# Stick-breaking attention woven into a projection and MLP: the weights are turned into the score banks, and the pieces are regrouped

## The chip, the cores and the metric

The kernel runs on one NeuronCore of a Trainium2 chip. A time is the device time in microseconds (us) of one execution. The kernel before was run three times: median 2823.44, from 2823.38 to 2826.13. The profile is that of a further execution, which took 2821.06 us.

## The reference

One inference step of a layer with 2048 prompt tokens and 64 new tokens, model width 1024, in float32. The tokens are normalised and projected to four groups of heads; group C is stick-breaking attention, the part that the change is about. For one head:

```
def sb_block(qb, qpos, k, v, kpos):
    z = jnp.einsum('bqhd,bkhd->bhqk', qb, k) * (SB_DH ** -0.5)
    mask = kpos[None, :] < qpos[:, None]
    ls_neg = jax.nn.log_sigmoid(-z)
    ls_pos = ls_neg + z
    lneg = jnp.where(mask, ls_neg, 0.0)
    rest = lax.cumsum(lneg, axis=3, reverse=True) - lneg
    w = jnp.where(mask, jnp.exp(ls_pos + rest), 0.0)
    return jnp.einsum('bhqk,bkhd->bqhd', w, v)
...
mix = jnp.concatenate([o_a, o_b, o_c, o_d], axis=-1) @ w_out
x = x + g1 * mix
h2 = rmsnorm(x, ln2_g) * (1.0 + sc2) + sh2
x = x + g2 * (jnp.square(jax.nn.relu(h2 @ mlp_w1)) @ mlp_w2)
```

A key's weight is the sigmoid of its score times the product of `1 - sigmoid` of all later keys, so a scan along the keys stands where other attention has a softmax. There are four heads of width 64.

## The kernel before, in words

The program has two phases. Phase one (input projection, the other head groups, the attention of the first 512 tokens) is not touched. Phase two, the function `tail_phase`, does the output projection and the MLP for four blocks of 512 tokens (the last one of 576, in two groups of 256 and 320 columns), and during the first three blocks the attention of the next block, two heads at a time.

**Strips and tiles.** A matrix product in float32 is made of three products of rounded halves, on 128x512 tiles. A tile of the output projection (`out`) or of the MLP's first matrix (`hid`) is a *strip* of 8 x 3 = 24 matmuls (L2400, L2401, L2404); a tile of the second matrix (`prj`) is 6 matmuls (L2442 to L2444), or 12 at a block's end (`prj2`, L2465 to L2467). Tiles take the four PSUM banks `dn` in turn: tile `u` is written in `dn[u % 4]`, and the function `bank` lets TensorE wait until tile `u - 4` has been read out. ScalarE reads `hid` tiles (L2074 a relu, L2076 a square, after which VectorE makes the low half, L2252 and L2254); VectorE reads the others, adding them to the residual (L2220).

**Slots.** The order is written out by hand. Each strip has 4 slots, a `prj` tile 1, a `prj2` tile 2, so that a slot is 6 matmuls. Each engine walks the same list of tiles and calls `step(slot)` as it passes a slot; TensorE does the attention's pieces of a slot behind the slot's 6 matmuls, the other engines do the steps of all slots of a tile before they read that tile out.

**A pair** is one tile of 128 queries (64 for the new tokens) against up to 512 keys, both heads; there are 76 pairs in 8 groups, and a group's last pair ends with its output. Pair `t` begins at slot `beta[t]`, one each 10.75 slots. From there, in slots:

| slot | engine | work |
|---|---|---|
| 0 | TensorE | `score`: both heads' scores into the two banks `sc` (L2317) |
| 2 | ScalarE | two sigmoids of `sc` (L1948, L1949) |
| 5 | VectorE | copy, two scans, copy, product: the weights `taken` (L2133 to L2142) |
| 10, 12 | TensorE | `turn`: head 0, head 1 transposed into the one bank `wt`, 4 each (L2329) |
| 11, 13 | ScalarE | `copy`: `wt` into `aT` (L1956), which frees `wt` |
| 14, 15 | TensorE | `values`: head 0, head 1, weights times values into the bank `ob`, 8 matmuls each (L2340) |
| 17 to 23 | all | after a group's last pair: copy out, head norms, `turn_out` (slot 22, L2350, into `wt`), copy |

So the eight PSUM banks are 4 `dn`, 2 `sc`, 1 `wt`, 1 `ob`. In block 0 the weights are split into halves on the way (ScalarE L1940, VectorE L2123, 128x1024 each); later blocks load the halves from memory.

Of the kernel before, what the change touches and what calls it, by code (L numbers as in the profile page):

```python
# [1477 lines left out]
def tail_phase(nc, const, x_v, o_v, q_v, k_v, sbv_p, sbv_s, cache_sb_v, w_out, mlp_w1, mlp_w2, y_prompt, y_sample):  # L1478
# [8 lines left out]
    HALF = 2 * P  # L1487
    PV, PA = "dve", "act"

    def groups(b):  # L1490
# [31 lines left out]

    SIG, SCAN, TURN, COPY, VALUES = 2, 5, (10, 12), (11, 13), (14, 15)
    FIN_OUT, FIN_STAT, FIN_SCALE, FIN_TURN, FIN_COPY = 17, 18, 20, 22, 23
    LEAD = 6
    beta = [LEAD + 43 * i // 4 for i in range(N_PAIRS)]
    at = {slot: t for t, slot in enumerate(beta)}
    at_last = {beta[t]: t for t in range(N_PAIRS) if pairs[t].last}
    past_piece = {beta[t]: pairs[t].piece for t in range(N_PAIRS) if t + 1 == N_PAIRS or pairs[t].piece != pairs[t + 1].piece}
    N_SLOTS = beta[-1] + FIN_COPY + 2  # L1530
# [153 lines left out]

    wt_no = {}
    for slot in range(N_SLOTS):
        if slot - FIN_TURN in at_last:
            wt_no["fin", pairs[at_last[slot - FIN_TURN]].group] = len(wt_no)
        for j in range(2):
            if slot - TURN[j] in at:  # L1690
                wt_no["turn", at[slot - TURN[j]], j] = len(wt_no)

# [11 lines left out]
    with ExitStack() as ctx:  # L1704
# [31 lines left out]
        stage = strips[0:6]  # L1736
        dn = [ps(f"dn{i}") for i in range(4)]
        sc, wt, ob = ps("sc", (P, 2, 512)), ps("wt"), ps("ob")

# [44 lines left out]
        def _(sp):  # L1784
# [77 lines left out]
            def step(slot):  # L1862

                n = past_piece.get(slot - VALUES[1] - 1)
# [67 lines left out]
        def _(act):  # L1932
# [9 lines left out]
            def sigmoids(t):  # L1942
                p = pairs[t]
                act.wait_ge(sc_full, t + 1)
                wait(act, w_ready, t)
                wait(act, wt_full, wt_no["turn", t - 2, 1] + 1 if t >= 2 else 0)
                z = sc[0:p.rows, :, 0:p.w]
                act.activation(left[0:p.rows, :, 0:p.w], z, ACT.Sigmoid, scale=-1.0)  # L1948
                act.activation(taken[t % 2][0:p.rows, :, 0:p.w], z, ACT.Sigmoid).then_inc(sig_ready, 1)  # L1949

            def copy(t, j):
                p = pairs[t]
                act.wait_ge(wt_full, wt_no["turn", t, j] + 1)
                wait(act, pv_done, 2 * (t - 1) + j + 1)
                n = p.nk * p.rows
                act.activation(aT[0:p.kr, j, 0:n], wt[0:p.kr, 0:n], ACT.Copy).then_inc(wt_read, 1)  # L1956

# [16 lines left out]
            def place(g):  # L1974

                b, j = attn_groups[g]
                act.wait_ge(wt_full, wt_no["fin", g] + 1)
                wait(act, o_lo, KT * min(b, NB - 1))
                a, n = (BLK, DEC) if b == NB else (0, BLK)
                act.activation(oC[:, j, a:a + n], wt[:, 0:n], ACT.Copy, scale=prm2[:, R2_ON + 4 + j:R2_ON + 5 + j]  # L1980
                               ).then_inc(wt_read, 1)

            def step(slot):
                t = at_last.get(slot - FIN_COPY)
                if t is not None:
                    place(pairs[t].group)
                for j in range(2):
                    t = at.get(slot - COPY[j])
                    if t is not None:
                        copy(t, j)  # L1990
                t = at.get(slot - SIG)
                if t is not None:
                    sigmoids(t)
                t = at_last.get(slot - FIN_STAT)
                if t is not None:
                    head_roots(t)
# [40 lines left out]
            def inverse_rms(kind, b, g):  # L2037
                u = tile_no["nsum" if kind == "second" else "fsum", b, g]
                act.preload_act_table_set(EXP_LN)
                a, e = groups(b)[g]  # L2040
                act.wait_ge(d_full, u + 1)
                act.activation(rms[:, a:e], dn[u % 4][:, 0:e - a], ACT.Ln, scale=1.0 / D_MODEL,
                               bias=eps[:, 0:1]).then_inc(evac[PA], 1)
                act.wait_ge(evac[PA], freed[u][1])
                act.activation(rms[:, a:e], rms[:, a:e], ACT.Exp, scale=-0.5).then_inc(n_rms, 1)
# [14 lines left out]
            def hidden(b, c, ft, g):  # L2060
# [11 lines left out]
                if c == 0:  # L2072
                    act.wait_ge(lo2, KT * (b + 1))
                act.activation(r, dn[u % 4][:, 0:e - a], ACT.Relu).then_inc(evac[PA], 1)  # L2074
                act.wait_ge(evac[PA], freed[u][1])
# [27 lines left out]
            def rows_of(b, i, v):  # L2103
# [3 lines left out]
                wait(act, y_out[n % 2], 16 * (n // 2))  # L2107
                act.activation(yrow[n % 2][0:rows, 0:512], dn[u % 4][0:rows, :], ACT.Copy).then_inc(evac[PA], 1)

# [5 lines left out]
        def _(dve):  # L2115
# [98 lines left out]
            def added(kind, mod, b, f, g, u):  # L2214
# [3 lines left out]
                for s, t, m in ranges(a, e):  # L2218
                    cols = xs[b % 2][:, f, s:t]
                    ins = dve.scalar_tensor_tensor(out=cols, in0=dn[u % 4][:, s - a:t - a], scalar=modT[:, mod + f, m:m + 1],  # L2220
                                                   in1=cols, op0=ALU.mult, op1=ALU.add)
# [86 lines left out]
        def _(pe):  # L2308
            def score(t):
                p = pairs[t]  # L2310
                q, k = qp[p.group % 2], kp[p.piece % 2]
                wait(pe, sig_ready, t)
                pe.wait_ge(q_in[p.group % 2], 16 * (p.group // 2 + 1))
# [10 lines left out]
            def turn(t, j):  # L2324
                p = pairs[t]
                pe.wait_ge(w_ready, t + 1)
                wait(pe, wt_read, wt_no["turn", t, j])
                for v in range(p.nk):
                    ins = pe.transpose(wt[0:p.kr, v * p.rows:(v + 1) * p.rows],  # L2329
                                       taken[t % 2][0:p.rows, j, v * p.kr:(v + 1) * p.kr], ident[0:p.rows, 0:p.rows])  # L2330
# [14 lines left out]
            def turn_out(t):  # L2345
# [3 lines left out]
                for s in range(1 if p.sample else TPB):  # L2349
                    ins = pe.transpose(wt[:, s * p.rows:(s + 1) * p.rows], osb[0:p.rows, s * P:(s + 1) * P],  # L2350
                                       ident[0:p.rows, 0:p.rows])
                ins.then_inc(wt_full, 1)

            def step(slot):
                for j in range(2):
                    t = at.get(slot - VALUES[j])
                    if t is not None:
# [4 lines left out]
                for j in range(2):  # L2362
                    t = at.get(slot - TURN[j])
                    if t is not None:
                        turn(t, j)
# [150 lines left out]
```

## Time and profile before

| what | value |
|---|---|
| time, median of 3 (range) | 2823.44 us (2823.38 to 2826.13) |
| time of the profiled execution, its span | 2821.06 us, 2819.3 us |
| TensorE busy | 2718.6 us, 96% |
| VectorE busy, ScalarE busy | 1459.5 us, 1075.1 us |
| phase two | from 788.8 us to the end |
| stretch of phase two with attention and at full clock | 872 to 2245 us |

A row of the timeline has the start of an instruction (or of several alike in a row, xN) and how long it took. Matmuls overlap: the time of a matmul is read from its start to the next one's start, not from its own length. Idle time and what ended it stand in square brackets.

### The profile page before, as it was taken

The page shows a single profiled execution, that of the slowest core. Times are in us where ns is not written, and L with a number is a line of the kernel's source. Part 1 is how long each engine was busy: PE and PEld are TensorE (multiplying, and loading weights), DVE is VectorE, ACT ScalarE, POOL GpSimd, SP SyncE. Part 2 cuts the span into 40 slices and gives each one's busy share as a digit, 9 for nine tenths or more (in the row PEclk, how much of TensorE's full clock was granted, in tenths as well). Part 3 has the DMA queues.
Part 4 walks back from the last instruction along what each step waited for, and adds up shares of the span by engine and source line. Part 5 has one row for each costly group of instructions (what it writes and reads, how often), then busy time and mean ns, then how long its engine had stood idle before and what let it go on. Part 6 is the DMA issues. An engine that isn't in the chain of part 4 may idle for free.

```text
span 2819.3 us, 36506 instructions
## 1 busy us (share of the span) xinstructions
PE 2718.6 (96%) x14669; PEld 2224.5 (79%) x14669; DVE 1459.5 (52%) x2315; ACT 1075.1 (38%) x1728; POOL 33.2 (1%) x43
## 2 busy tenths in 40 slices
PE   7999999999978999999999999999999999999996
PEld 2589777777766777777787878777777788999996
DVE  4455563554436657665564455555545434544553
ACT  3374846656434343433433322343222322221112
POOL 0000000000000000000000000001000000100000
PEclk9999999999989999999999999999999999999999
DMA  9533435324386676775435454534453643454441
GB/s 338 174 105 114 115 113 153 113 83 135 101 282 244 221 243 227 238 253 206 147 138 192 179 185 164 191 127 172 151 204 140 216 180 135 165 177 166 166 179 64
DMA packets 285934, 485.99 MB, mean 172 GB/s; under 512 B 21963, under 2 KB 168326, under 8 KB 285766
## 3 DMA queue, kind: packets, MB, share of 16 engines
q1 hardware_dynamic: 279526, 471.07, 48.7%
q10 hardware_dynamic: 6240, 12.58, 1.2%
q8 instruction: 118, 1.93, 0.3%
q14 instruction: 50, 0.41, 0.0%
HBM read 374.52 MB, written 109.06 MB: 172 GB/s over the span
## 4 chain that ended last, share of the span: by engine, by line
PE 62%; DVE 5%; ACT 2%; DMA 2%; issue 1%; SPq 1%; DVEq 0%; ACTq 0%
PE t_dn L2400 10%; PE t_dn L2404 10%; PE t_dn L2401 10%; PE t_dn L2442 7%; PE t_dn L2444 7%; PE t_dn L2443 7%; PE t_ob L2340 3%; PE t_sc L2317 2%; PE t_wt L2329 2%; DVE t_left L2137 1%; PE t_dn L2465 1%; PE t_dn L2467 1%; PE t_dn L2466 1%; DVE t_xs L2220 1%; DMA ring_lo<-lo_scratch 1%
## 5 line engine op out<-in xcount | busy, mean ns | idle before, releaser
L2400 PE MATMUL t_dn<-t_h_hi,ring_hi 128*128 128x512 f32 (+2 forms) x1600 | 588.0, 368 | 18.0 <-ACT t_h_hi L2027 7.1
L2220 DVE SCALAR_TENSOR_TENSOR t_xs<-t_dn,modT,t_xs 128x512 f32<-128x512 f32 (+2 forms) x768 | 422.5, 580 | 312.9 <-PE t_dn L2444 167.6
L2404 PE MATMUL t_dn<-t_h_lo,ring_hi 128*128 128x512 f32 (+2 forms) x1600 | 568.9, 356 | 3.8 <-DVE t_h_lo L2202 3.4
L2401 PE MATMUL t_dn<-t_h_hi,ring_lo 128*128 128x512 f32 (+2 forms) x1600 | 566.6, 354 | 0.0
L2442 PE MATMUL t_dn<-t_g_hi,t_w2h 128*128 128x512 f32 (+2 forms) x1120 | 412.3, 368 | 11.5 <-DVE t_xs L2220 9.3
L2444 PE MATMUL t_dn<-t_g_lo,t_w2h 128*128 128x512 f32 (+2 forms) x1120 | 396.6, 354 | 0.0
L2443 PE MATMUL t_dn<-t_g_hi,t_w2l 128*128 128x512 f32 (+2 forms) x1120 | 395.7, 353 | 0.0
L2252 DVE TENSOR_TENSOR t_rt<-t_rt 128x512 f32<-128x512 f32 (+2 forms) x160 | 95.8, 599 | 551.1 <-ACT t_g_hi L2076 551.1
L2400 PEld LDWEIGHTS t_dn<-t_h_hi,ring_hi 128*128 128x128 f32 x1600 | 304.2, 190 | 75.3 <-issue 32.1
L2404 PEld LDWEIGHTS t_dn<-t_h_lo,ring_hi 128*128 128x128 f32 x1600 | 303.3, 190 | 47.8 <-DVE t_h_lo L2202 6.9
L2401 PEld LDWEIGHTS t_dn<-t_h_hi,ring_lo 128*128 128x128 f32 x1600 | 304.5, 190 | 31.4 <-issue 0.5
L2074 ACT ACTIVATE t_rt<-t_dn 128x512 f32<-128x512 f32 (+2 forms) x160 | 83.7, 523 | 639.5 <-PE t_dn L2404 639.5
L1447 PE MATMUL f_zr<-hn_hi,ring_hi 128*128 128x512 f32 (+1 forms) x880 | 319.3, 363 | 6.5 <-ACT f_gb L897 2.6
L1449 PE MATMUL f_zr<-hn_hi,ring_lo 128*128 128x512 f32 (+1 forms) x880 | 309.9, 352 | 0.0
L1448 PE MATMUL f_zr<-hn_lo,ring_hi 128*128 128x512 f32 (+1 forms) x880 | 309.4, 352 | 0.0
L2442 PEld LDWEIGHTS t_dn<-t_g_hi,t_w2h 128*128 128x128 f32 x1120 | 211.9, 189 | 53.4 <-DVE t_xs L2220 20.6
L2444 PEld LDWEIGHTS t_dn<-t_g_lo,t_w2h 128*128 128x128 f32 x1120 | 211.7, 189 | 28.0
L1956 ACT ACTIVATE t_aT<-t_wt 128x512 f32<-128x512 f32 (+4 forms) x152 | 80.2, 528 | 398.9 <-PE t_wt L2329 398.8
L2443 PEld LDWEIGHTS t_dn<-t_g_hi,t_w2l 128*128 128x128 f32 x1120 | 212.3, 190 | 20.6
L1089 DVE TENSOR_TENSOR ring_lo<-f_wraw,ring_hi 128x1024 fp32r<-128x1024 f32 x90 | 110.1, 1224 | 215.8 <-ACT ring_hi L864 215.6
L1447 PEld LDWEIGHTS f_zr<-hn_hi,ring_hi 128*128 128x128 f32 x880 | 165.2, 188 | 39.4 <-issue 12.9
L864 ACT ACTIVATE ring_hi<-f_wraw 128x1024 fp32r<-128x1024 f32 x90 | 94.9, 1055 | 240.1 <-PE f_zr L1449 215.7
(344 smaller groups left out, 3426.1 us busy)
## 6 DMA issues: line engine op xcount, KB each, us to landing
ring_hi<-hi_scratch SPq DMA_DIRECT2D x120, 512.0 KB, 4.0
ring_lo<-lo_scratch SPq DMA_DIRECT2D x120, 512.0 KB, 4.9
t_w2h<-hi_scratch SPq DMA_DIRECT2D x96, 512.0 KB, 6.1
t_w2l<-lo_scratch SPq DMA_DIRECT2D x96, 512.0 KB, 7.1
f_wraw<-in_w_in_dram SPq DMA_DIRECT2D x88, 512.0 KB, 3.9
t_raw<-in_mlp_w_dram SPq DMA_DIRECT2D x64, 512.0 KB, 4.7
hi_scratch<-ring_hi SPq DMA_DIRECT2D x40, 512.0 KB, 5.6
lo_scratch<-ring_lo SPq DMA_DIRECT2D x40, 512.0 KB, 6.3
```

Of the source, the lines that this page charges most:

```text
L1089: dve.tensor_tensor(w_lo[n % 2][:, :, :], wraw[n % 2][:, :, :], w_hi[n % 2][:, :, :].bitcast(F32), ALU.subtract).then_inc(w_lo_ok, 1)
L1447: pe.matmul(out, wh, hi, start=(k == 0), stop=False)
L1448: pe.matmul(out, wh, lo, start=False, stop=False)
L1449: ins = pe.matmul(out, wl, hi, start=False, stop=(k == KT - 1))
L2220: ins = dve.scalar_tensor_tensor(out=cols, in0=dn[u % 4][:, s - a:t - a], scalar=modT[:, mod + f, m:m + 1], in1=cols, op0=ALU.mult, op1=AL ...
L2252: dve.tensor_tensor(r, r, r, ALU.mult).then_inc(g_sq, 1)
L2400: pe.matmul(out, hi[:, k, :], h_hi[:, k, a:e], start=(i == 0), stop=False)
L2401: pe.matmul(out, lo[:, k, :], h_hi[:, k, a:e], start=False, stop=False)
L2404: ins = pe.matmul(out, hi[:, k, :], h_lo[:, k, a:e], start=False, stop=(i == KT - 1))
L2442: pe.matmul(out[:, 0:e - a], hi[:, d, :], g_hi[c % 2][:, ft, a:e], start=(ft == 0), stop=False)
L2443: pe.matmul(out[:, 0:e - a], lo[:, d, :], g_hi[c % 2][:, ft, a:e], start=False, stop=False)
L2444: ins = pe.matmul(out[:, 0:e - a], hi[:, d, :], g_lo[c % 2][:, ft, a:e], start=False, stop=(ft == 1))
```

## The change

The bank `wt` is given up. Both heads' weights are transposed in one piece, at slot 8, head `j` into its own score bank `sc[:, j]`, which the sigmoids have read by then; ScalarE copies both from there at slot 9. The values of a pair are done, both heads in one piece, right before the scores of the next pair (slot 10 or 11); that score now waits until the copies have read `sc` (semaphore `wt_read`). Sigmoids move from slot 2 to 1, the scan from 5 to 3. The sigmoids' wait for the turn of pair `t - 2` is gone, being implied. The freed bank becomes a fifth `dn`. Pairs come each 10.5 slots instead of 10.75; after a group's last pair three slots are put in, two pairs later, and the group's output is turned at slot 21 into `sc[:, 0]`. The loading of keys and values moves with the values.

```diff
+    NDN = 5
...
-    SIG, SCAN, TURN, COPY, VALUES = 2, 5, (10, 12), (11, 13), (14, 15)
-    FIN_OUT, FIN_STAT, FIN_SCALE, FIN_TURN, FIN_COPY = 17, 18, 20, 22, 23
-    LEAD = 6
-    beta = [LEAD + 43 * i // 4 for i in range(N_PAIRS)]
+    SIG, SCAN, TURN, COPY, VALUES = 1, 3, 8, 9, 11
+    FIN_OUT, FIN_STAT, FIN_SCALE, FIN_TURN, FIN_COPY = 12, 13, 17, 21, 22
+    LEAD, FIN_GAP = 6, 3
+    beta = [LEAD + 21 * i // 2 + FIN_GAP * sum(p.last for p in pairs[:max(i - 1, 0)]) for i in range(N_PAIRS)]
+    values_at = {beta[t + 1] if t + 1 < N_PAIRS else beta[t] + VALUES: t for t in range(N_PAIRS)}
...
-        dn = [ps(f"dn{i}") for i in range(4)]
-        sc, wt, ob = ps("sc", (P, 2, 512)), ps("wt"), ps("ob")
+        dn = [ps(f"dn{i}") for i in range(NDN)]
+        sc, ob = ps("sc", (P, 2, 512)), ps("ob")
...
                 act.wait_ge(sc_full, t + 1)
                 wait(act, w_ready, t)
-                wait(act, wt_full, wt_no["turn", t - 2, 1] + 1 if t >= 2 else 0)
...
-                act.activation(aT[0:p.kr, j, 0:n], wt[0:p.kr, 0:n], ACT.Copy).then_inc(wt_read, 1)
+                act.activation(aT[0:p.kr, j, 0:n], sc[0:p.kr, j, 0:n], ACT.Copy).then_inc(wt_read, 1)
...
             def score(t):
-                wait(pe, sig_ready, t)
+                wait(pe, wt_read, wt_before[t])
...
             def turn(t, j):
                 pe.wait_ge(w_ready, t + 1)
-                wait(pe, wt_read, wt_no["turn", t, j])
                 for v in range(p.nk):
-                    ins = pe.transpose(wt[0:p.kr, v * p.rows:(v + 1) * p.rows],
+                    ins = pe.transpose(sc[0:p.kr, j, v * p.rows:(v + 1) * p.rows],
...
             def step(slot):
-                for j in range(2):
-                    t = at.get(slot - VALUES[j])
-                    if t is not None:
+                t = values_at.get(slot)
+                if t is not None:
+                    for j in range(2):
                         values(t, j)
...
             def bank(u):
-                if u >= 4:
-                    by, done = freed[u - 4]
+                if u >= NDN:
+                    by, done = freed[u - NDN]
                     pe.wait_ge(evac[by], done)
-                return dn[u % 4]
+                return dn[u % NDN]
```

Two places show what moves. On TensorE, pairs 62 to 64 (third block; `t_kp` are keys, `t_vp` values). The marks stand for strip and tile matmuls alone. Before, there are 6 of them behind the first turn, 6 behind the score, 12 behind the second turn, 6 and 36 behind the two pieces of values:

```order
L2329 MATMUL t_wt<-ident,t_taken 128x128 x4
...
L2317 MATMUL t_sc<-t_kp,t_qp 128x512 x2
...
L2329 MATMUL t_wt<-ident,t_taken 128x128 x4
...
L2340 MATMUL t_ob<-t_vp,t_aT 128x64 x4
...
L2340 MATMUL t_ob<-t_vp,t_aT 128x64 x4
```

After the change, in the same place, 48 of them stand between a score and the turn, and 12 or 18 between the turn and the next values:

```order
L2330 MATMUL t_sc<-ident,t_taken 128x128 x8
...
L2341 MATMUL t_ob<-t_vp,t_aT 128x64 x8
L2319 MATMUL t_sc<-t_kp,t_qp 128x512 x2
```

Five pieces have become two, and the score follows the values without a strip between them. (One `x4` of values is eight instructions on the chip, and `x2` of scores four.)

On VectorE, pair 23 (block 0; the scan is listed as a SCALAR_TENSOR_TENSOR of `t_left`). Before, from the end of the pair's `hid` tile:

```order
L2252 TENSOR_TENSOR t_rt<-t_rt 128x512
L2254 TENSOR_TENSOR t_g_lo<-t_rt,t_g_hi 128x512
L2123 TENSOR_TENSOR ring_lo<-t_raw,ring_hi 128x1024
L2220 SCALAR_TENSOR_TENSOR t_xs<-t_dn,modT,t_xs 128x512 x2
L2133 COPY t_left<-t_carry 128x2
L2137 SCALAR_TENSOR_TENSOR t_left<-t_left 128x512 x2
L2141 COPY t_carry<-t_left 128x2
L2142 TENSOR_TENSOR t_taken<-t_taken,t_left 128x1024
L2220 SCALAR_TENSOR_TENSOR t_xs<-t_dn,modT,t_xs 128x512 x2
```

After:

```order
L2254 TENSOR_TENSOR t_rt<-t_rt 128x512
L2256 TENSOR_TENSOR t_g_lo<-t_rt,t_g_hi 128x512
L2125 TENSOR_TENSOR ring_lo<-t_raw,ring_hi 128x1024
L2135 COPY t_left<-t_carry 128x2
L2139 SCALAR_TENSOR_TENSOR t_left<-t_left 128x512 x2
L2143 COPY t_carry<-t_left 128x2
L2144 TENSOR_TENSOR t_taken<-t_taken,t_left 128x1024
L2222 SCALAR_TENSOR_TENSOR t_xs<-t_dn,modT,t_xs 128x512 x4
```

The scan has moved ahead of two tiles that VectorE reads out (L2220, now L2222); these now come behind it.

## Rows read from the trace of the kernel before

**Rows 1.** The attention stretch: length; busy us of PE, PEld, DVE, ACT, POOL; clock; DMA.

```profile
872.00:2245.00 1373.00, 1357.08 (x6696) 1077.47 (x6697) 752.10 (x1054) 476.80 (x776) 19.99 (x14) 1.00 0.54 191
```

**Rows 2.** TensorE's waits from 780 us: total, times, longest.

```profile
PE t_dn L2442 <- DVE t_xs L2220: 9.3, 12, 1.2
...
PE t_wt L2350 <- ACT t_aT L1956: 3.1, 2, 2.6
...
PE t_dn L2442 <- ACT strips L2108: 2.1, 1, 2.1
PE t_wt L2350 <- DVE t_osb L2157: 1.8, 1, 1.8
...
PE t_wt L2329 <- ACT t_aT L1956: 0.7, 1, 0.7
```

**Rows 3.** TensorE's timeline: a turn, then a score, between strips.

```profile
1502.96 0.40 PE L2404 MATMUL t_dn<-t_h_lo,ring_hi 128*128 128x512 f32 x1
1503.19 0.60 PE L2329 MATMUL t_wt<-ident,t_taken 128*128 128x128 f32 x4
...
1503.86 0.40 PE L2401 MATMUL t_dn<-t_h_hi,ring_lo 128*128 128x512 f32 x1
...
1504.79 0.40 PE L2404 MATMUL t_dn<-t_h_lo,ring_hi 128*128 128x512 f32 x1
1505.12 1.13 PE L2317 MATMUL t_sc<-t_kp,t_qp 64*128 64x512 f32 x4
1506.18 0.50 PE L2400 MATMUL t_dn<-t_h_hi,ring_hi 128*128 128x512 f32 x1
1506.51 0.39 PE L2401 MATMUL t_dn<-t_h_hi,ring_lo 128*128 128x512 f32 x1
```

**Rows 4.** The transposes by their line: ns of one, least/median/most.

```profile
L2329 PE MATMUL t_wt<-ident,t_taken x524: 222/272/415, 826.5 to 2259.0; 128*128 128x128 f32 x168, 64*128 64x64 f32 x6, 64*64 64x64 f32 x1
```

**Rows 5.** TensorE's timeline: one head's values between strips.

```profile
1510.66 0.40 PE L2404 MATMUL t_dn<-t_h_lo,ring_hi 128*128 128x512 f32 x1
1510.89 1.00 PE L2340 MATMUL t_ob<-t_vp,t_aT 128*128 128x64 f32 x8
...
1512.02 0.39 PE L2401 MATMUL t_dn<-t_h_hi,ring_lo 128*128 128x512 f32 x1
...
1512.93 0.40 PE L2404 MATMUL t_dn<-t_h_lo,ring_hi 128*128 128x512 f32 x1
```

**Rows 6.** TensorE's timeline: turn and score in one piece (first, last row of four).

```profile
1522.00 0.39 PE L2444 MATMUL t_dn<-t_g_lo,t_w2h 128*128 128x512 f32 x1
...
1524.16 0.40 PE L2443 MATMUL t_dn<-t_g_hi,t_w2l 128*128 128x512 f32 x1
```

**Rows 7.** ScalarE's timeline, same pair.

```profile
1508.31 0.60 ACT L1956 ACTIVATE t_aT<-t_wt 128x512 f32<-128x512 f32 x1 [3.88 <-PE t_wt L2329]
1508.80 1.02 ACT L1948 ACTIVATE t_left<-t_sc 128x1024 f32<-128x1024 f32 x1
...
1510.61 0.62 ACT L2074 ACTIVATE t_rt<-t_dn 128x512 f32<-128x512 f32 x1
```

**Rows 8.** VectorE's timeline, same pair.

```profile
1511.92 0.69 DVE L2252 TENSOR_TENSOR t_rt<-t_rt 128x512 f32<-128x512 f32 x1 [9.61 <-ACT t_g_hi L2076]
...
1513.25 0.16 DVE L2133 COPY t_left<-t_carry 128x2 f32<-128x2 f32 x1
...
1516.02 1.22 DVE L2142 TENSOR_TENSOR t_taken<-t_taken,t_left 128x1024 f32<-128x1024 f32 x1
```

**Rows 9.** VectorE's timeline, pair 23 (block 0).

```profile
1261.71 1.22 DVE L2123 TENSOR_TENSOR ring_lo<-t_raw,ring_hi 128x1024 fp32r<-128x1024 f32 x1
...
1264.16 0.16 DVE L2133 COPY t_left<-t_carry 128x2 f32<-128x2 f32 x1
...
1268.07 1.40 DVE L2220 SCALAR_TENSOR_TENSOR t_xs<-t_dn,modT,t_xs 128x512 f32<-128x512 f32 x2
```

**Rows 10.** TensorE's timeline, same time as rows 9.

```profile
1268.86 0.50 PE L2442 MATMUL t_dn<-t_g_hi,t_w2h 128*128 128x512 f32 x1 [0.74 <-DVE t_xs L2220]
```

More of the change, by code:

```diff
@@ L1520, in tail_phase @@
     N_PAIRS = len(pairs)
-    SIG, SCAN, TURN, COPY, VALUES = 2, 5, (10, 12), (11, 13), (14, 15)
-    FIN_OUT, FIN_STAT, FIN_SCALE, FIN_TURN, FIN_COPY = 17, 18, 20, 22, 23
-    LEAD = 6
-    beta = [LEAD + 43 * i // 4 for i in range(N_PAIRS)]
+    SIG, SCAN, TURN, COPY, VALUES = 1, 3, 8, 9, 11
[3 more added lines that the diff above has]
+    values_at = {beta[t + 1] if t + 1 < N_PAIRS else beta[t] + VALUES: t for t in range(N_PAIRS)}
     at = {slot: t for t, slot in enumerate(beta)}
     at_last = {beta[t]: t for t in range(N_PAIRS) if pairs[t].last}
-    past_piece = {beta[t]: pairs[t].piece for t in range(N_PAIRS) if t + 1 == N_PAIRS or pairs[t].piece != pairs[t + 1].piece}
+    past_piece = {slot: pairs[t].piece for slot, t in values_at.items() if t + 1 == N_PAIRS or pairs[t].piece != pairs[t + 1].piece}
     N_SLOTS = beta[-1] + FIN_COPY + 2
@@ L1682, in freed_by @@
         return full("hid", old[1], old[2], old[3], last_group(old[1]))
-    wt_no = {}
+    wt_no, wt_before = {}, {}
     for slot in range(N_SLOTS):
@@ L1688, in tail_phase @@
             wt_no["fin", pairs[at_last[slot - FIN_TURN]].group] = len(wt_no)
-        for j in range(2):
-            if slot - TURN[j] in at:
-                wt_no["turn", at[slot - TURN[j]], j] = len(wt_no)
+        for j in range(2 if slot - TURN in at else 0):
+            wt_no["turn", at[slot - TURN], j] = len(wt_no)
+        if slot in at:
+            wt_before[at[slot]] = len(wt_no)
     class Slots:
@@ L1862, in step @@
             def step(slot):
-                n = past_piece.get(slot - VALUES[1] - 1)
+                n = past_piece.get(slot - 1)
                 if n is not None and n + 2 < len(pieces):
@@ L1979, in place @@
                 a, n = (BLK, DEC) if b == NB else (0, BLK)
-                act.activation(oC[:, j, a:a + n], wt[:, 0:n], ACT.Copy, scale=prm2[:, R2_ON + 4 + j:R2_ON + 5 + j]
+                act.activation(oC[:, j, a:a + n], sc[:, 0, 0:n], ACT.Copy, scale=prm2[:, R2_ON + 4 + j:R2_ON + 5 + j]
                                ).then_inc(wt_read, 1)
@@ L1986, in step @@
                     place(pairs[t].group)
-                for j in range(2):
-                    t = at.get(slot - COPY[j])
-                    if t is not None:
+                t = at.get(slot - COPY)
+                if t is not None:
+                    for j in range(2):
                         copy(t, j)
@@ L2041, in inverse_rms @@
                 act.wait_ge(d_full, u + 1)
-                act.activation(rms[:, a:e], dn[u % 4][:, 0:e - a], ACT.Ln, scale=1.0 / D_MODEL,
+                act.activation(rms[:, a:e], dn[u % NDN][:, 0:e - a], ACT.Ln, scale=1.0 / D_MODEL,
                                bias=eps[:, 0:1]).then_inc(evac[PA], 1)
@@ L2073, in hidden @@
                     act.wait_ge(lo2, KT * (b + 1))
-                act.activation(r, dn[u % 4][:, 0:e - a], ACT.Relu).then_inc(evac[PA], 1)
+                act.activation(r, dn[u % NDN][:, 0:e - a], ACT.Relu).then_inc(evac[PA], 1)
                 act.wait_ge(evac[PA], freed[u][1])
@@ L2107, in rows_of @@
                 wait(act, y_out[n % 2], 16 * (n // 2))
-                act.activation(yrow[n % 2][0:rows, 0:512], dn[u % 4][0:rows, :], ACT.Copy).then_inc(evac[PA], 1)
+                act.activation(yrow[n % 2][0:rows, 0:512], dn[u % NDN][0:rows, :], ACT.Copy).then_inc(evac[PA], 1)
             for i in range(KT):
@@ L2219, in added @@
                     cols = xs[b % 2][:, f, s:t]
-                    ins = dve.scalar_tensor_tensor(out=cols, in0=dn[u % 4][:, s - a:t - a], scalar=modT[:, mod + f, m:m + 1],
+                    ins = dve.scalar_tensor_tensor(out=cols, in0=dn[u % NDN][:, s - a:t - a], scalar=modT[:, mod + f, m:m + 1],
                                                    in1=cols, op0=ALU.mult, op1=ALU.add)
@@ L2349, in turn_out @@
                 for s in range(1 if p.sample else TPB):
-                    ins = pe.transpose(wt[:, s * p.rows:(s + 1) * p.rows], osb[0:p.rows, s * P:(s + 1) * P],
+                    ins = pe.transpose(sc[:, 0, s * p.rows:(s + 1) * p.rows], osb[0:p.rows, s * P:(s + 1) * P],
                                        ident[0:p.rows, 0:p.rows])
@@ L2354, in step @@
             def step(slot):
-                for j in range(2):
-                    t = at.get(slot - VALUES[j])
-                    if t is not None:
+                t = values_at.get(slot)
+                if t is not None:
+                    for j in range(2):
                         values(t, j)
@@ L2361, in step @@
                     turn_out(t)
-                for j in range(2):
-                    t = at.get(slot - TURN[j])
-                    if t is not None:
+                t = at.get(slot - TURN)
+                if t is not None:
+                    for j in range(2):
                         turn(t, j)
```

## The prediction

> **What bounds the kernel now.** I read the page first, then the busy time by stretches, TensorE's waits, and last the timelines of single pieces. The page gives a span of 2819.3 us, with TensorE busy for 96% of it (the table above); the attention can only cost or give what changes on TensorE. All 76 pairs lie, but for the first few, in the stretch from 872 to 2245 us. There TensorE is busy for 1357.08 of 1373 us at a granted clock of 1.00 [rows 1], so at most 15.9 us can come from idle time; the rest would have to come from TensorE's own work getting shorter. The waits say where the idle time is: 9.3 us in 12 pieces before the first matmul of a `prj` tile, released by VectorE's read-out of an older tile (a wait for a bank, longest 1.2); 3.1 and 1.8 us before a group's output is turned; 0.7 before a turn; and 2.1 us in the last block, where a bank waits for ScalarE's copy of finished rows [rows 2]. So I have two accounts: the price of the pieces, and the waits.
>
> **The price of the pieces.** The matmuls are the same in number and shape; what changes is how they stand together. Unbroken strip matmuls follow each other every 0.2275 us (four from 1512.02 to 1512.93 [rows 5]), a slot of six thus takes 1.365. A turn of one head: from the strip matmul before it, 1502.96, to the second one behind it, 1503.86, is 0.90, less two strip intervals 0.455: 0.445 [rows 3]. A score in the same way: 1.72 - 0.455 = 1.265 [rows 3]. Values of one head: 1.36 - 0.455 = 0.905 [rows 5].
>
> Does a joint save anything? Inside a turn, matmuls start every (0.60 - 0.27) / 3 = 0.11 us: four take 0.60 [rows 3], one 0.27 [rows 4]; four more in the same piece add 0.44 to 0.445, the price of a piece by itself. So joining the turns saves about 0.01. The eight values take 1.00 together [rows 5], 0.104 from one to the next by the same reckoning, or 0.113 if the 0.905 is spread evenly; eight more add 0.83 to 0.905: 0 to 0.07 saved. For values and score in one piece there is no row; the nearest is a turn and a score in one piece, which some pairs of the kernel before have: 2.16 - 0.455 = 1.705 against 0.445 + 1.265 = 1.71 [rows 6]. That saves 0.005; at the other end I allow this joint 0.07 as well. I take 0.01 + 0.02 + 0.01 = 0.04 per pair, nearest to the row of a real joint: 76 x 0.04 = **3 us**, with ends 0 and 76 x 0.15 = 11.
>
> The Trainium skill, "TensorE: Matmul & The Clock Gate", section on LDWEIGHTS, gives a weight load as columns / 1.2 ns, 107 ns for 128 columns, however few columns then move. By that rule every matmul of a piece costs one load, joined or not, and joining gives 0: my sum would be 3 us smaller. The pitch of 0.11 us [rows 3, 4] agrees with it; the values' row leaves a little room, which is why I keep the 3.
>
> **Bank waits.** A fifth bank lets TensorE run one tile further, 1.365 us for `prj`, more than the longest of the 12 waits (1.2). Alone that would remove all 9.3. But the pieces move too. Before, between a scan and the bank's reuse stood the second turn and two values, 0.445 + 1.81 = 2.26 us of TensorE's work in which VectorE caught up; now eight bare slots stand there. The worst case is a scan right behind a `hid` tile, the next `prj` tiles waiting behind it. From ScalarE's relu to the end of VectorE's two steps is 1513.25 - 1510.61 = 2.64 [rows 7, 8]; in block 0 the low half of the weights adds up to 1.22; copy and scans and product take 1268.07 - 1264.16 = 3.91; the read-out then releases TensorE 1268.86 - 1268.07 = 0.79 later [rows 9, 10]. Together 7.34, in block 0 8.56, against five tiles, 6.83: a wait of 0.5 or 1.7. Each `prj` tile read before the scan adds 0.70 to VectorE (two take 1.40 [rows 9]) and 1.365 to TensorE, so one of them leaves -0.2 or 1.0. Worked out from `beta` and the slots of the tiles, the scan follows a pair of `hid` tiles with no tile between in pair 23, with one in pairs 17 and 20 (all in block 0) and in 38, 71 and 75. For those with one, ScalarE's sigmoids (1510.61 - 1508.80 = 1.81 [rows 7]) hold the relu back up to 0.5 more. Sum: 1.7 + 2 x 1.3 + 3 x 0.3 = 5.2. Bank waits thus go from 9.3 to about 5: **4 us** gained, with ends -2 and 9.3.
>
> **The group's end.** From the last values to the output's turn there were 7 slots and are now 10 or 11: 3 x 1.365 = 4.1 us more, and the longest of these three waits is 2.6 [rows 2]. All **4.9 us** go. ScalarE's norms and VectorE's scaling, which were late, have this time; the output's turn waits for nothing newer, since pair `t + 1` was copied two slots earlier.
>
> **Turns and the new wait.** A turn no longer waits for `wt`: **1 us**. In its place the score, with it everything behind it on TensorE, waits for two copies. A copy takes 0.49 (to the next instruction [rows 7]), two about 1; TensorE has two slots (2.73) or three in between, so the cover holds unless ScalarE is more than 1.7 us behind, as in block 0 where it also rounds weights. I book **-1.5 us** for such cases, ends 0 and -5.
>
> **Scan against turn.** The turn moves from slot 10 to 8, and no pieces stand before it: 2 x 1.365 + 2.26 = 5.0 us earlier after its score. The scan's slot moves from 5 to 3 past the same pieces: 5.0 us earlier too. In the pair of [rows 3, 8] VectorE ended at 1516.02 + 1.22, 11.1 us after TensorE went back to strips (1506.18), and the turn is now due 8 x 1.365 = 10.9 us after. If VectorE follows, it is ready near 6 and nothing waits; the sigmoids, which stood behind the first copy, can now start right after the score. The queue that loads keys and values waits for the values one slot later as before; nothing changes for it.
>
> **The last block** has no attention; of its 2.1 us the fifth bank can take one tile, which is shorter there: **1 us**.
>
> **Sum.** 3 + 4 + 4.9 + 1 + 1 - 1.5 = 12.4 us, against the profiled execution 2821.06 - 12.4 = 2808.7. The median of the runs lies 2.4 above that execution: **2811**.
>
> **Rivals.** *Everything pays* (chance 0.14): the bank waits vanish, as 1.365 against 1.2 says, and joints save 7, half way to their upper end. Then 12.4 + 5 + 4 = 21 us: 2802. For it speaks the row of the waits; against it, eight bare slots.
>
> *The waits move house* (0.17): joints save nothing, bank waits stay at 9, scores wait for copies up to the -5. What is left is 4.9 + 1 + 1 - 5 = 2: 2821. For it: the real joint saves 0.005 [rows 6].
>
> *The turn comes too early* (0.10), the slower one. If VectorE's queue does not let the scan move up, the weights of that pair come 0.2 us late, and those of pair 23, whose scan began at 1264.16, much later. At more than 12.4 / 76 = 0.16 us per pair all is eaten; at 0.5 a pair the time is 2823.4 - 12.4 + 38 = 2849. Against it: VectorE is busy 752 of 1373 us [rows 1], and the order shows the scan moved up.
>
> **How the numbers follow.** The forecast, a gain of 6 to 18 us, has 0.59: 2805 to 2817. The range reaches a little past the first rival, to 2799, and past the second, to 2822; outside are the slower rival and the tails of these two, 0.2. Within 0.2%, 5.6 us, a measurement of this kernel can hardly tell from no change. Faster by more than that: nearly all of the forecast and the first rival, 0.73. Same: the second, 0.17. Slower: the third, 0.10.
>
> **What would show it.** Right: 0.44 us for each four transposes in a piece of eight; no wait before the output's turn; bank waits on VectorE near 5 us, at pairs 17, 20 and 23; no wait of a turn on VectorE's product. Wrong: waits before `turn` or `score` of tenths in most pairs; bank waits as long as before; or a busy time of TensorE in the attention stretch lower by much more than 3 us.

## The result, and the profile after

The changed kernel takes 2796.24 us (median of 4 runs, 2795.57 to 2798.32), the kernel before in the same comparison 2823.41: a ratio of 0.9904, interval 0.9887 to 0.9921. The forecast had the direction, faster, and less than half of the size: 27 us instead of 12.4, and the time lies below the range. The sums below set one profiled execution against the other: 2795.57 (span 2793.8) against 2821.06, 25.5 us. Of these, 24.9 lie in the three blocks with attention, from the last norm sum before them (L2421, now L2422) to the last one at their end: 859.1 to 2347.6 us before, 860.4 to 2324.0 after. This stretch will be used again, because the rest moves by itself: phase one, which no edit touches, ends between 788.7 and 792.7 us in the profiled executions of this document (788.8 before, 788.7 after), and the last block takes 466.5 to 471.7. Line numbers are one or two higher than before.

The same stretch as in [rows 1], in the changed kernel; the columns are the same:

```profile
872.00:2245.00 1373.00, 1365.14 (x6810) 1107.40 (x6811) 760.69 (x1069) 482.99 (x790) 19.88 (x14) 1.00 0.55 194
```

TensorE stands idle for 7.9 us instead of 15.9, and 114 more matmuls fit into the same time. So in this stretch idle time is about a third of the gain; the larger part is work of TensorE that became shorter, which the forecast had named among the signs of its being wrong. TensorE's waits from 780 us, to be held against [rows 2]:

```profile
PE t_dn L2485 <- DVE t_xs L2297: 10.2, 2, 7.6
...
PE t_dn L2443 <- DVE t_xs L2222: 3.3, 4, 1.7
...
PE t_dn L2485 <- DVE t_xs L2222: 1.4, 1, 1.4
...
PE t_dn L2443 <- ACT strips L2110: 0.9, 1, 0.9
PE t_sc L2330 <- DVE t_taken L2144: 0.8, 1, 0.8
...
PE t_ob L2341 <- ACT t_aT L1958: 0.2, 1, 0.2
```

The reader is to see three things. The waits before the output's turn (3.1 and 1.8 before) have no row any more. The waits for a bank on VectorE's read-out went from 9.3 to 3.3 + 1.4. And the new wait, values and scores for ScalarE's copies, is 0.2 us in one place. The two longest bank waits stand where they were forecast, in pairs 20 and 23 (TensorE's timeline, one row for each):

```profile
1205.70 0.50 PE L2443 MATMUL t_dn<-t_g_hi,t_w2h 128*128 128x512 f32 x1 [1.28 <-DVE t_xs L2222]
...
1261.56 0.50 PE L2443 MATMUL t_dn<-t_g_hi,t_w2h 128*128 128x512 f32 x1 [1.70 <-DVE t_xs L2222]
```

VectorE's timeline ahead of the second of them:

```profile
1255.72 1.22 DVE L2125 TENSOR_TENSOR ring_lo<-t_raw,ring_hi 128x1024 fp32r<-128x1024 f32 x1
1256.86 0.16 DVE L2135 COPY t_left<-t_carry 128x2 f32<-128x2 f32 x1
...
1259.63 1.22 DVE L2144 TENSOR_TENSOR t_taken<-t_taken,t_left 128x1024 f32<-128x1024 f32 x1
1260.77 2.72 DVE L2222 SCALAR_TENSOR_TENSOR t_xs<-t_dn,modT,t_xs 128x512 f32<-128x512 f32 x4
```

From the scan's start to the first read-out 1260.77 - 1256.86 = 3.91, and TensorE goes on 0.79 later: the terms of [rows 9, 10], and the wait is 1.70 where 1.7 was worked out.

The pieces now, on TensorE's timeline: a turn of two heads, and values and scores in one piece.

```profile
1656.10 0.39 PE L2405 MATMUL t_dn<-t_h_lo,ring_hi 128*128 128x512 f32 x1
1656.33 1.03 PE L2330 MATMUL t_sc<-ident,t_taken 128*128 128x128 f32 x8
1657.12 0.48 PE L2401 MATMUL t_dn<-t_h_hi,ring_hi 128*128 128x512 f32 x1
1657.43 0.40 PE L2402 MATMUL t_dn<-t_h_hi,ring_lo 128*128 128x512 f32 x1
...
1659.71 0.40 PE L2405 MATMUL t_dn<-t_h_lo,ring_hi 128*128 128x512 f32 x1
1659.94 1.90 PE L2341 MATMUL t_ob<-t_vp,t_aT 128*128 128x64 f32 x16
1661.77 1.13 PE L2319 MATMUL t_sc<-t_kp,t_qp 64*128 64x512 f32 x4
1662.83 0.50 PE L2401 MATMUL t_dn<-t_h_hi,ring_hi 128*128 128x512 f32 x1
1663.16 0.39 PE L2402 MATMUL t_dn<-t_h_hi,ring_lo 128*128 128x512 f32 x1
...
1665.20 0.39 PE L2402 MATMUL t_dn<-t_h_hi,ring_lo 128*128 128x512 f32 x1
```

By the reckoning of the forecast the turn is 1.33 - 0.455 = 0.875 against 2 x 0.445, and the joint piece 3.45 - 0.455 = 2.995 against 2 x 0.905 + 1.265 = 3.075 in [rows 3, 5]. Medians over all full pieces of a trace, from the starts with a strip interval of 0.2266, say it more exactly: turns 0.884 against 2 x 0.450; values and scores 3.000 against 2 x 0.910 + 1.269 = 3.089. The forecast had 0.03 for this piece; it is 0.09 by these medians. One thing more is in these rows: from 1663.16 to 1665.20 nine strips take 2.04, 0.2267 each, the undisturbed interval. Why that is worth a sentence comes below.

### The profile page after: what moved, and what is told of

Same layout as the page of the kernel before. It is cut to its first block, busy times and chain, and to the rows that moved or that the text cites. A ratio compares the mean times of both kernels' runs of the same rounds, so it can differ in the third digit from the quotient of the medians.

```text
span 2793.8 us, 36355 instructions
## 1 busy us (share of the span) xinstructions
PE 2706.6 (97%) x14669; PEld 2240.4 (80%) x14669; DVE 1458.2 (52%) x2315; ACT 1074.0 (38%) x1728; POOL 33.1 (1%) x43
## 4 chain that ended last, share of the span: by engine, by line
PE 65%; DVE 3%; DMA 2%; ACT 1%; issue 1%; SPq 0%; DVEq 0%; ACTq 0%
PE t_dn L2401 10%; PE t_dn L2405 10%; PE t_dn L2402 10%; PE t_dn L2443 7%; PE t_dn L2445 7%; PE t_dn L2444 7%; PE t_ob L2341 4%; PE t_sc L2319 3%; PE t_sc L2330 2%; PE t_dn L2466 1%; PE t_dn L2468 1%; PE t_dn L2467 1%; DVE t_left L2139 1%; DMA out_dram<-strips 1%; DMA lo_scratch<-ring_lo 1%
## 5 line engine op out<-in xcount | busy, mean ns | idle before, releaser
L2401 PE MATMUL t_dn<-t_h_hi,ring_hi 128*128 128x512 f32 (+2 forms) x1600 | 578.6, 362 | 19.2 <-DVE ring_lo L2125 8.2
L2222 DVE SCALAR_TENSOR_TENSOR t_xs<-t_dn,modT,t_xs 128x512 f32<-128x512 f32 (+2 forms) x768 | 420.7, 580 | 313.2 <-PE t_dn L2445 176.5
L2443 PE MATMUL t_dn<-t_g_hi,t_w2h 128*128 128x512 f32 (+2 forms) x1120 | 402.8, 360 | 4.2 <-DVE t_xs L2222 3.3
L2444 PEld LDWEIGHTS t_dn<-t_g_hi,t_w2l 128*128 128x128 f32 x1120 | 211.5, 189 | 23.6
L2139 DVE TENSOR_TENSOR_SCAN t_left<-t_left 128x512 f32<-128x512 f32 (+5 forms) x152 | 166.1, 1134 | 41.9 <-ACT t_taken L1951 39.4
```

Source lines behind the costliest of these rows:

```text
L2139: ins = dve.tensor_tensor_scan(keep[:, j, ::-1], keep[:, j, ::-1], keep[:, j, ::-1], upto[:, j:j + 1], ALU.mult, ALU.min)
L2222: ins = dve.scalar_tensor_tensor(out=cols, in0=dn[u % NDN][:, s - a:t - a], scalar=modT[:, mod + f, m:m + 1], in1=cols, op0=ALU.mult, op1= ...
L2401: pe.matmul(out, hi[:, k, :], h_hi[:, k, a:e], start=(i == 0), stop=False)
L2443: pe.matmul(out[:, 0:e - a], hi[:, d, :], g_hi[c % 2][:, ft, a:e], start=(ft == 0), stop=False)
L2444: pe.matmul(out[:, 0:e - a], lo[:, d, :], g_hi[c % 2][:, ft, a:e], start=False, stop=False)
```

## The experiments

**Which joint is worth what.** In the kernel before, the values of both heads in one piece, apart from the scores:

```diff
-    SIG, SCAN, TURN, COPY, VALUES = 2, 5, (10, 12), (11, 13), (14, 15)
+    SIG, SCAN, TURN, COPY, VALUES = 2, 5, (10, 12), (11, 13), (15, 15)
```

> The kernel before with one part of the change alone: the values of both heads in one piece, in slot 15 instead of 14 and 15, apart from the scores. It prices the joint of values and values by itself. If a joint saves a fixed re-entry into the strips wherever the pieces are small, 0.03 to 0.07 us per pair: 2 to 5 us shorter than the kernel before, 2818 to 2821. By the forecast's middle value of 0.02 it is 1.5 us shorter, 2822; by the rule of weight loads it is the same. In the last two cases the larger part of the saving must come from values and score in one piece.

Measured: 2814.95 us, ratio 0.9972 (0.9960 to 0.9983), 8 us less than before and less than any of the expected times; the three blocks are 7.0 shorter. The joint is the smaller part of it: sixteen values take 1.803 against 2 x 0.910, 0.017 per pair or 1.3 us. The bank waits on VectorE's read-out fell by more, from 9.3 to 5.8 us. The likely reason, not tested apart, is that one head's values came a slot later and VectorE had that time. The forecast's 0.02 for this joint holds; the larger part of the time goes with a place, not with a joint.

In the changed kernel, the values behind the next scores, still one piece:

```diff
-    values_at = {beta[t + 1] if t + 1 < N_PAIRS else beta[t] + VALUES: t for t in range(N_PAIRS)}
+    values_at = {beta[t + 1] + 1 if t + 1 < N_PAIRS else beta[t] + VALUES: t for t in range(N_PAIRS)}
-    FIN_OUT, FIN_STAT, FIN_SCALE, FIN_TURN, FIN_COPY = 12, 13, 17, 21, 22
+    FIN_OUT, FIN_STAT, FIN_SCALE, FIN_TURN, FIN_COPY = 13, 14, 17, 21, 22
```

> The changed kernel with the values of both heads one slot behind the next scores, still one piece of sixteen matmuls, and the group's end one slot later to match. If the joint of values and scores is worth what the pieces show (3.000 us joined against 2 x 0.910 + 1.269 = 3.089 apart, of which the joint of the two heads' values is the smaller part), it costs 0.05 to 0.09 us in each of 76 pairs: 4 to 7 us longer than the changed kernel, 2800 to 2803, and values and score apart take 3.05 to 3.09. By the rule that every matmul costs its weight load, joined or not, nothing: 2796 within 1 us, unless waits change.

Measured: 2799.10, ratio 0.9912 (0.9899 to 0.9926). This interval and that of the changed kernel overlap, so the time alone decides nothing; the pieces do. Values take 1.798, scores 1.259: 3.057 apart against 3.000 joined. The joint of values and scores is worth **0.057 us**, 4.3 us over 76 pairs. And the strips behind the values changed:

```profile
1665.66 1.89 PE L2341 MATMUL t_ob<-t_vp,t_aT 128*128 128x64 f32 x16
1667.37 0.47 PE L2401 MATMUL t_dn<-t_h_hi,ring_hi 128*128 128x512 f32 x1
1667.68 0.39 PE L2402 MATMUL t_dn<-t_h_hi,ring_lo 128*128 128x512 f32 x1
...
1669.76 0.39 PE L2402 MATMUL t_dn<-t_h_hi,ring_lo 128*128 128x512 f32 x1
```

The second strip starts 0.31 behind the first, and the nine after it take 2.08, 0.231 each instead of 0.2267. I call strips that follow the one before by more than 0.2285 and less than 0.26 us *late strips* (the expectations call them slow), and count those of 512 columns from 863 to 2745 us: 1264 in the kernel before, 521 in the changed one, 1086 here. What they add over 0.2266 is 8.0, 3.2 and 6.4 us. So 4.8 us of the saving between before and after are late strips, which were in no term of the forecast.

The same piece turned round, scores first, to see which end of it saves:

```diff
+                t = at.get(slot)
+                if t is not None:
+                    score(t)
                 t = values_at.get(slot)
...
-                t = at.get(slot)
-                if t is not None:
-                    score(t)
```

> The changed kernel with the piece turned round: in the slot of the values and the next scores the four score matmuls come first and the sixteen values behind them. If what is saved is the way from small values back into the strips (the second strip behind values starts 0.09 us late, and up to ten strips after it run at 0.224 to 0.236 us instead of 0.2266), it comes back: 0.05 us per pair in the piece and about 2 us in slow strips, 5 to 7 us longer than the changed kernel, 2801 to 2803, with over 900 slow strips. If any joint saves the same whichever end meets the strips, the piece takes 3.00 and the time is 2796 to 2798; the sigmoids start 1.8 us earlier, which can change single bank waits by a few tenths each.

Measured: 2799.76, ratio 0.9915 (0.9901 to 0.9929); the piece takes 3.046, with 930 late strips (5.4 us). Of the 0.057 only 0.011 is left when the values meet the strips. So most of the saving is the way out of the values, from the last value back into the strips.

The turns apart again:

```diff
-    SIG, SCAN, TURN, COPY, VALUES = 1, 3, 8, 9, 11
+    SIG, SCAN, TURN, COPY, VALUES = 1, 3, (8, 9), 9, 11
...
-                t = at.get(slot - TURN)
-                if t is not None:
-                    for j in range(2):
+                for j in range(2):
+                    t = at.get(slot - TURN[j])
+                    if t is not None:
                         turn(t, j)
```

> The changed kernel with the two heads turned in two slots, 8 and 9, both copies in slot 9; values and scores as they are. If a joint of two turns is worth what the pieces show (0.884 joined against 2 x 0.450), 76 x 0.016 = 1.2 us longer; and if strips run slower because transposes stood before them, and not because of what ScalarE does at that time, the strips over 0.2285 us apart rise from 514 towards 800 or more and cost another 1 to 2 us: 2797 to 2800. If turns and slow strips carry nothing, 2796 within 0.5 us, with about 500 slow strips.

Measured: 2801.32 (2797.34 to 2803.75 over 4 runs), ratio 0.9920 (0.9907 to 0.9934); the three blocks are 4.7 longer than in the changed kernel. A turn of one head is 0.451 again, two 0.902 against 0.884; late strips are 856 (5.4 us, 2.2 more).

What makes strips late? One theory was the distance to the piece before:

```diff
-    values_at = {beta[t + 1] if t + 1 < N_PAIRS else beta[t] + VALUES: t for t in range(N_PAIRS)}
+    values_at = {beta[t + 1] + 2 if t + 1 < N_PAIRS else beta[t] + VALUES: t for t in range(N_PAIRS)}
-    FIN_OUT, FIN_STAT, FIN_SCALE, FIN_TURN, FIN_COPY = 12, 13, 17, 21, 22
+    FIN_OUT, FIN_STAT, FIN_SCALE, FIN_TURN, FIN_COPY = 14, 15, 17, 21, 22
```

> The changed kernel with the values two slots behind the next scores (one slot in the run before), in one piece, the group's end two slots later to match. It asks what makes strips slow. If the distance to the piece before counts, twelve strips instead of six between scores and values, the slow strips fall from 1086 towards 600 and the time by 2 to 3 us against one slot behind, to 2796 or 2797. If values by themselves leave eight slow strips whatever stands ahead, they stay at about 1000 and the time at 2799 within 1.5 us, unless waits change.

Measured: 2796.18, ratio 0.9902 (0.9888 to 0.9917); 963 late strips. Neither theory holds. The values now leave one late strip in most places instead of seven or eight, as distance would have it; but scores alone leave seven or eight of the twelve strips behind them late, and the piece before them is twelve strips or more away. Scores with sixteen values ahead of them leave none. The time is that of the changed kernel although its pieces (1.803 + 1.259 = 3.062) and late strips cost 7.0 us more, 4.7 + 5.5 - 3.2. Part of this came back as waits that went away: no bank wait on VectorE's read-out and no turn's wait for the product is left in this trace.

How well these parts account for the four kernels shows in the three blocks. All figures are us against the changed kernel; the waits are those of TensorE for VectorE's read-outs and products and for ScalarE's copies (5.7 in the changed kernel: 3.3 + 1.4 + 0.8 + 0.2):

| kernel | pieces | late strips | waits | sum | three blocks, measured |
|---|---|---|---|---|---|
| values one slot behind | 4.3 | 3.2 | -2.7 | 4.8 | 4.3 |
| scores first | 3.5 | 2.2 | -0.5 | 5.2 | 5.3 |
| turns apart | 1.4 | 2.2 | -0.2 | 3.4 | 4.7 |
| values two slots behind | 4.7 | 2.3 | -3.7 | 3.3 | 2.9 |

The sums come within 1.3 us of what was measured.

**The waits.** The group's end alone, in the kernel before:

```diff
-    FIN_OUT, FIN_STAT, FIN_SCALE, FIN_TURN, FIN_COPY = 17, 18, 20, 22, 23
+    FIN_OUT, FIN_STAT, FIN_SCALE, FIN_TURN, FIN_COPY = 17, 18, 20, 25, 26
```

> The kernel before with one part of the change alone: the turn and the copy of a group's output three slots later (25 and 26). The term of the sum for the group's end says that all of the 4.9 us of waits ahead of this turn go, and nothing newer is waited for: 4 to 5 us shorter than the kernel before, 2818 to 2820. If another wait takes their place (a turn of the weights bank behind it, or VectorE later), 2822 to 2824.

Measured: 2818.57, 4.9 us less than the kernel before, ratio 0.9981 (0.9972 to 0.9990). Of these waits, 4.9 us, 0.4 is left; but a turn's wait for the weights bank grew from 0.7 to 1.9, and the bank waits on VectorE from 9.3 to 9.9. By the waits the edit thus gives 2.7 us; the three blocks are 4.0 shorter. That the time fell by just the 4.9 of the term is in part chance: its interval goes from 2.8 to 7.9 us.

The changed kernel without the fifth bank, then with sigmoids and scan in their old slots, then with both edits:

```diff
-    NDN = 5
+    NDN = 4
```

```diff
-    SIG, SCAN, TURN, COPY, VALUES = 1, 3, 8, 9, 11
+    SIG, SCAN, TURN, COPY, VALUES = 2, 5, 8, 9, 11
```

> The changed kernel with four banks for strips and tiles; the seventh bank stays unused. If the fifth bank is the cover that the eight bare slots need, each tile loses 1.37 us of it: the waits on VectorE's read-outs, 3.3 us in the changed kernel, grow by 1.37 in pairs 17, 20, 23, 38, 71 and 75 and by less in others, to 11 to 16 us, the last block loses about 1 us more, and the kernel takes 8 to 14 us longer than the changed one, 2804 to 2810. If the pieces' new places alone removed the bank waits, it takes at most 3 us longer, 2796 to 2799, with bank waits below 5 us.

> The changed kernel with sigmoids and scan in the slots that they had before, 2 and 5, and the turn in slot 8 as changed. It sizes the slower rival, the turn that comes too early. Two more prj tiles are read before the scan: the product ends up to 2 x 0.70 = 1.4 us later in pairs among prj tiles, more behind a hid tile. Products end 3 to 11.4 us after the scores in the changed kernel, and the turn is due 11.0 after. By that, some 10 pairs wait, 0.3 to 2 us each: 5 to 15 us longer, 2801 to 2811; the rival's 0.5 us in each of 76 pairs would give 2834. If bank waits fall by as much (fewer read-outs stand behind the scan), the time stays within 3 us.

> The changed kernel with both taken back: four banks, and sigmoids and scan in slots 2 and 5. Each alone cost 22 to 24 us: without the fifth bank 18.9 us of waits for banks, with the scan late 23.6 us of waits of the turn for its product and no wait for a bank. If the two are separate prices, the pieces' new order without either is 2835 to 2845, slower than the kernel before. If they are one price paid in two places (the fifth bank only buys the room for the early scan, and a late scan needs no fifth bank), it is 2818 to 2823, with turns waiting some 24 us and banks under 4 us.

| kernel | time | ratio to before |
|---|---|---|
| changed: five banks, scan in slot 3 | 2796.24 | 0.9904 (0.9887 to 0.9921) |
| four banks, scan in slot 3 | 2818.42 | 0.9983 (0.9974 to 0.9992) |
| five banks, scan in slot 5 | 2819.83 | 0.9986 (0.9977 to 0.9995) |
| four banks, scan in slot 5 | 2831.43 | 1.0025 (1.0014 to 1.0035) |

TensorE's waits with four banks:

```profile
PE t_dn L2443 <- DVE t_xs L2222: 15.9, 9, 3.1
...
PE t_dn L2401 <- DVE t_xs L2222: 3.0, 2, 1.9
...
PE t_dn L2443 <- ACT strips L2110: 1.3, 1, 1.3
```

with the late scan:

```profile
PE t_sc L2330 <- DVE t_taken L2144: 23.6, 18, 3.3
```

and with both:

```profile
PE t_sc L2330 <- DVE t_taken L2144: 23.2, 18, 3.2
...
PE t_dn L2443 <- DVE t_xs L2222: 4.4, 3, 1.7
...
PE t_dn L2401 <- DVE t_xs L2222: 0.9, 2, 0.5
```

Set against the kernel with both taken back, the early scan alone gains 13.0 us, the fifth bank alone 11.6, and both together 35.2. So each is worth 12 to 13 us alone and 22 to 24 where the other is there: some 10 us come only with both. The last two prices are above what was expected (8 to 14 and 5 to 15). With the early scan and four banks, 18.9 us are waited for banks, twice the 9.3 of before; the reading of the forecast, that the values no longer stand between the scan and the reuse of the bank, fits this but was not tested apart. With five banks and the late scan no wait on a read-out is left, but 18 turns wait 23.6 us for their product. With both taken back the kernel is slower than before, by less than two separate prices (2842) and more than one (2820): there the turns wait 23.2 us, and in that time VectorE frees banks, so that bank waits are 5.3 us instead of 18.9.

These views do not hold the whole difference. Between the profiled executions of four and of five banks, 22.4 us, the bank waits are 18.9 - 4.7 = 14.2, and 2.7 lie in phase one, which the edit does not touch (it ends at 791.4 instead of 788.7). Another part is TensorE's clock. With four banks, behind the longest wait:

```profile
1271.41 0.80 PE L2443 MATMUL t_dn<-t_g_hi,t_w2h 128*128 128x512 f32 x1 [3.07 <-DVE t_xs L2222]
1272.00 0.63 PE L2444 MATMUL t_dn<-t_g_hi,t_w2l 128*128 128x512 f32 x1
1272.43 0.63 PE L2445 MATMUL t_dn<-t_g_lo,t_w2h 128*128 128x512 f32 x1
```

The same time by stretch (the columns are those of [rows 1]):

```profile
1271.30:1274.60 3.30, 3.19 (x8) 2.52 (x9) 3.30 (x6) 0.00 (x0) 0.00 (x0) 0.50 0.47 192
```

The granted clock is 0.50 there, the lower of its two levels (1.2 instead of 2.4 GHz), and strips follow each other every 0.43 us instead of 0.2266. The same stands behind a wait of 2.47 us, from 1496.6 to 1499.9. An estimate from the starts of the matmuls in both places is 3 us. The changed kernel has no such stretch between 872 and 2245 us; with the late scan there are two, with both edits four. So these waits of TensorE cost more than their own length. The rest, about 2.5 us, I did not assign. In the last block four banks have 1.3 us of waits for ScalarE's copy, five 0.9; from the first norm sum at the end of the blocks before to the end both take 470 us (469.8 and 470.5).

**Is there more to get?** The scan one slot later, 4 instead of 3 (the first new line), and then the turn one slot later too, with the copies in its slot (the second):

```diff
-    SIG, SCAN, TURN, COPY, VALUES = 1, 3, 8, 9, 11
+    SIG, SCAN, TURN, COPY, VALUES = 1, 4, 8, 9, 11
+    SIG, SCAN, TURN, COPY, VALUES = 1, 4, 9, 9, 11
```

> The changed kernel with the scan alone one slot later, 4 instead of 3. The two longest bank waits left (1.9 and 1.5 us, pairs 23 and 20) stand behind a scan right behind a hid tile; with one prj tile read before the scan they should shrink by about 1.4 us minus 0.7 each, while products end up to 0.7 us later and the turns of pairs 3, 20, 23 and 51 (products 10.4 to 11.4 us after the scores, the turn due at 11.0) wait up to 0.7. By that it is 2794 to 2797. If instead every wait of the bank comes from the whole of VectorE's work, nothing moves; if the turn has no room, 2798 to 2802.

> The changed kernel with the scan one slot later (4) and the turn one slot later (9), the copies in slot 9 behind it. With the scan in slot 4 alone the waits for a bank on VectorE went from 4.7 to 0.3 us and the turns' waits for the product from 0.8 to 5.1 (6 pairs, longest 1.0); one slot more, 1.37 us, covers all six. If nothing takes their place, both kinds are gone and the kernel is 3 to 5 us shorter than the changed one, 2791 to 2793. If the copies now end too late for the values and scores, which stand one slot behind the turn in every second pair, there are waits of tenths in up to 38 pairs, and the time is 2796 to 2805.

Measured: 2796.99, ratio 0.9900 (0.9886 to 0.9914), and 2798.23, ratio 0.9911 (0.9894 to 0.9927). Neither beats the changed kernel. With the scan in slot 4 the bank waits fell to 0.3 us, and turns wait 5.1; with the turn later the turns wait for nothing, and the bank waits are back at 5.2. Three of the waits stand at the same places of the program. First two turns of the kernel with the scan in slot 4:

```profile
1042.40 0.44 PE L2330 MATMUL t_sc<-ident,t_taken 128*128 128x128 f32 x2 [0.99 <-DVE t_taken L2144]
...
1098.97 0.33 PE L2330 MATMUL t_sc<-ident,t_taken 128*128 128x128 f32 x1 [1.04 <-DVE t_taken L2144]
```

and then, with the turn in slot 9, the two tiles that come where those turns were:

```profile
1041.89 0.50 PE L2443 MATMUL t_dn<-t_g_hi,t_w2h 128*128 128x512 f32 x1 [1.65 <-DVE t_xs L2222]
...
1099.09 0.50 PE L2443 MATMUL t_dn<-t_g_hi,t_w2h 128*128 128x512 f32 x1 [1.71 <-DVE t_xs L2222]
```

By these places, VectorE is late there with the same work, and which of its results TensorE asks for first gives the wait its name (and not quite its length: 0.99 and 1.04 against 1.65 and 1.71). That "one slot more covers all six" was wrong for this reason. The kernel with the turn in slot 9 also has a wait of 1.9 us for the low half of a strip (`t_h_lo`), and behind it the clock is 0.50 from 1287.6 to 1291.0.

## Why the prediction was right in direction and too small

| term | forecast | measured |
|---|---|---|
| joints | 3 | 6.8: (0.057 + 0.017 + 0.016) x 76 |
| late strips | not seen | 4.8: 8.0 - 3.2 |
| bank waits | 4 | 4.6: 9.3 - 3.3 - 1.4 |
| group's end | 4.9 | 4.9 |
| turn, new wait | 1 - 1.5 | 0.1: 0.7 + 0.4 before, 0.8 + 0.2 after |
| last block | 1 | 1.9, four banks gain as much |
| sum | 12.4 | 23.1 of 25.5 |

**The step that failed** is the price of the pieces, in the sentence that takes a turn and a score as the nearest row for values and score: 0.01 per pair, where 0.057 was measured. What counts is the way out of the piece that is joined, and that stood in the trace of the kernel before. The median from the last transpose of a turn to the start of the next strip is 0.028 us, from the last value 0.084; the strip behind that starts 0.316 and 0.317 later. Into a score both go alike, 0.202 from a transpose (kernel before) and 0.205 from a value (changed kernel). So a value's way out into strips is 0.056 us longer, as much as the joint saves; the real joint of [rows 6] could not show it, since its first part is a turn. The upper end that I had allowed, 0.15 per pair and 11 us for all joints, holds the 6.8. Two smaller terms of the same step were read too coarsely: the rows for two turns give 0.445 - 0.44 = 0.005 and not the 0.01 that was booked (measured 0.016), and values start 0.111 us apart in that trace, not 0.104.

The other half of the same step is that a piece was priced from the strip before it to the second strip behind it. By that window the late strips that follow were left out, though they stand in the row that I used for the strip interval: 0.2275 from [rows 5], where undisturbed strips take 0.2266.

The Trainium skill, "TensorE: Matmul & The Clock Gate", section on LDWEIGHTS, has a weight load take its columns / 1.2 ns, for 128 columns an estimated 0.107 us. The trace agrees inside a piece: sixteen values start 0.112 us apart, eight transposes 0.109. That joining gives nothing, as the prediction worked out from it, does not come true at the ends of a piece, by the 0.057.

**Right:** bank waits of about 5 (4.7), with the forecast's 1.7 in pair 23 and 1.3 in pair 20; none in pair 17, where one was expected, and one of 1.4 before a tile of finished rows, where none was. All waits of the group's end went in the changed kernel (alone, all but 0.4). No score waits, and values wait in one place; the -1.5 for copies was too careful by 1.3. The last block gained, but four banks gain as much there, so the reason given for that term is refuted; the largest part of the 1.9 is a wait for VectorE at the very end (11.7 before, 10.2 after), which lies between 10.2 and 11.2 in all other runs.

**The rivals.** "Everything pays" came nearest with its 2802, and its 7 for the joints meets the measured 6.8; but that 7 was half way to an upper end and no mechanism, and the bank waits, which were to vanish, did not. "The waits move house" is what the scan in slot 4 and the turn in slot 9 show, for some 5 us and not for all. "The turn comes too early" did not occur, but its condition is real: with the scan where it was, the kernel loses 24 us, 0.31 per pair, twice the 0.16 at which the rival was to decide; with four banks besides it is slower than before. About 2.4 us of the difference are not assigned. Part of them is the joints again: by the medians of the two kernels alone, values and scores save 0.089, which makes (0.089 + 0.016) x 76 = 8.0 instead of 6.8. A score starts among late strips in the kernel before and takes 1.269; with the values one slot behind it does not, and takes 1.259.

## What to carry to other kernels

Price a joint by the way out of the very piece that is to be joined (last small matmul, next strip, the strip behind it), and look at the ten strips that follow, not at two. When a stage is moved earlier past other work, the buffers between the engines belong to the move: without the earlier scan or without the fifth bank the new order gained 0.2% on the kernel before, with both 1%. A wait that a change removes on an engine that is late anyway can come back at the next thing asked of that engine; count what the late engine has to do, not the waits.

## What was not expected of the hardware

After some pieces the strips do not return to their interval at once: starts follow at 0.314, 0.235, 0.233, 0.236, 0.224, 0.231, 0.236, 0.228, 0.232, 0.231 and then 0.2266 us, the same series again and again, and pieces that disturb less enter it at a later place (two late strips behind eight transposes, none behind values and scores). In the kernel with the values one slot behind, 23% of the intervals between strips are late while VectorE, ScalarE and GpSimd are all idle (175 of 763), 22% while VectorE reads a tile out (224 of 1041), and 22% with those engines idle and no DMA transfer running either (74 of 344), at a granted clock of 1.00. So the series does not need the other engines' work. Scores alone start it, scores with sixteen values ahead do not; why is open.
